# Column order and placement of the operands of the feed-forward matmuls

## The reference, cut to what matters

```
D_MODEL = 2048; SEQ = 512; D_FF = 5632
h = rms_norm(x, norm_ffn[layer])
x = x + (jax.nn.silu(h @ w_gate[layer]) * (h @ w_up[layer])) @ w_down[layer]
return rms_norm(x, norm_final)
```

## Time and profile before

| | |
|---|---|
| median of the runs of the kernel before | 2104.19 us (2 runs, 2094.29 to 2114.09) |
| the profiled execution, its own time | 2099.91 us |
| its span in the trace | 2098.2 us |
| mean granted TensorE clock | 0.99 |
| TensorE matmul busy | 2040.7 us (97%) |
| VectorE busy | 1566.1 us (75%) |
| ScalarE busy | 956.3 us (46%) |

### The profile page before, as it was taken

One profiled execution on the slowest core, in us unless ns is written; L12 is line 12 of the kernel. 1 busy time (PEld: TensorE's weight loads), 2 busy tenths in 40 slices (PEclk: granted clock), 3 DMA queues, 4 the chain that ended last, 5 costly groups with the idle time before them and its releaser, 6 DMA issues.

```text
span 2098.2 us, 32169 instructions
## 1 busy us (share of the span) xinstructions
PE 2040.7 (97%) x13205; PEld 1817.0 (87%) x13205; DVE 1566.1 (75%) x2106; ACT 956.3 (46%) x1476; POOL 277.1 (13%) x153
## 2 busy tenths in 40 slices
PE   8999999999979999999999999999999999999998
PEld 6888777777658889999999999999999988888886
DVE  6723566777762227888898889889888898988995
ACT  5222356667652227544444444444444433333343
POOL 4000011211120000123113203203203100000002
PEclk9999999999989999999999999999999999999999
DMA  7671222211035334335446445345345755665622
GB/s 262 217 208 61 61 66 56 61 56 53 13 121 186 115 121 140 102 131 179 154 141 198 134 159 192 122 157 185 131 147 186 301 194 188 228 213 181 236 106 81
DMA packets 197779, 306.46 MB, mean 146 GB/s; under 512 B 8640, under 2 KB 121344, under 8 KB 192512
## 3 DMA queue, kind: packets, MB, share of 16 engines
q1 hardware_dynamic: 197600, 304.38, 43.6%
q10 hardware_dynamic: 32, 0.01, 0.0%
HBM read 248.79 MB, written 55.57 MB: 145 GB/s over the span
## 4 chain that ended last, share of the span: by engine, by line
PE 88%; DVE 6%; issue 3%; ACT 2%; DMA 0%; POOL 0%; DVEq 0%; ACTq 0%; POOLq 0%
PE bank L2641 11%; PE bank L2644 11%; PE bank L2646 11%; PE bank L2698 6%; PE bank L2696 6%; PE bank L2693 6%; PE bank L2242 3%; PE bank L2244 3%; PE bank L2243 3%; PE bank L2508 3%; PE bank L2510 3%; PE bank L2512 3%; PE bank L2408 3%; PE bank L2530 2%; PE bank L2534 2%
## 5 line engine op out<-in xcount | busy, mean ns | idle before, releaser
L1297 ACT ACTIVATE w_all<-raw 128x1024 fp32r<-128x1024 f32 x292 | 305.6, 1058 | 279.6 <-PE bank L2698 156.9
L1891 DVE TENSOR_TENSOR w_all<-raw,w_all 128x1024 fp32r<-128x1024 f32 x292 | 378.0, 1306 | 71.5 <-ACT w_all L1297 71.0
L2641 PE MATMUL bank<-x_T,w_all 128*128 128x256 f32 x1344 | 373.2, 278 | 0.0
L2646 PE MATMUL bank<-x_T,w_all 128*128 128x256 f32 x1344 | 373.2, 278 | 0.0
L2644 PE MATMUL bank<-x_T,w_all 128*128 128x256 f32 x1344 | 373.2, 278 | 0.0
L2641 PE MATMUL bank<-x_B,w_all 128*128 128x256 f32 x1008 | 280.9, 279 | 0.8 <-DVE w_all L1891 0.2
L2644 PE MATMUL bank<-x_B,w_all 128*128 128x256 f32 x1008 | 279.9, 278 | 0.0
L2646 PE MATMUL bank<-x_B,w_all 128*128 128x256 f32 x1008 | 279.9, 278 | 0.0
L2641 PEld LDWEIGHTS bank<-x_T,w_all 128*128 128x128 f32 x1344 | 254.2, 189 | 0.0
L2644 PEld LDWEIGHTS bank<-x_T,w_all 128*128 128x128 f32 x1344 | 252.3, 188 | 0.0
L2646 PEld LDWEIGHTS bank<-x_T,w_all 128*128 128x128 f32 x1344 | 252.3, 188 | 0.0
(11 more groups left out here) (299 smaller groups left out, 4394.3 us busy)
## 6 DMA issues: line engine op xcount, KB each, us to landing
raw<-in_w_gate SPq DMA_DIRECT2D x39, 1024.0 KB, 5.1
h_scratch<-late SPq DMA_DIRECT2D x70, 512.0 KB, 3.1
raw<-in_w_down SPq DMA_DIRECT2D x50, 512.0 KB, 5.2
proj_q<-in_w_up SPq DMA_DIRECT2D x22, 1024.0 KB, 6.8
raw<-in_w_up SPq DMA_DIRECT2D x22, 1024.0 KB, 7.9
x_B<-h_scratch SPq DMA_DIRECT2D x20, 1024.0 KB, 5.0
raw<-in_w_in SPq DMA_DIRECT2D x16, 1024.0 KB, 10.4
raw<-in_w_out SPq DMA_DIRECT2D x16, 1024.0 KB, 5.5
```

The source lines that it names most:

```text
L1297: nc.scalar.activation(piece_hi(p), piece_raw(n, k), ACT.Copy).then_inc(piece_hi_done, 1)
L1891: nc.vector.tensor_tensor(piece_lo(p), piece_raw(n, k), piece_hi(p).bitcast(F32), ALU.subtract).then_inc(piece_lo_done, 1)
L2641: nc.tensor.matmul(dst, wh[:, t, cs], x_lo(x)[:, cols], start=start and part == 0 and t == 0 and a == 0, stop=False, skip_group_check=True)
L2646: done = nc.tensor.matmul(dst, wh[:, t, cs], x_hi(x)[:, cols], start=False, stop=part == 1 and t == 3, skip_group_check=True)
```

## The change

`X_AT` gets a value of its own for each activation operand, and `h_flat(r)` a shift `H_AT[r]`. The accumulators of `sums` move from column 0 to column 128 of their halves, and so does the low part of the last down products. Two tables give each product an order in which the streamed columns are read; the PSUM columns are written in the same order, so each result stays in its place. Of every 256 or 512 columns, "lines" takes 16 from the first half, 16 from the second, then the next 16 of the first, and so on; "far" takes 16 from each of four quarters in turn; "halves" takes 8 from each half in turn; "plain" is the order of before. `first_piece`, `last_down` and all else keep the plain order; `first_piece` reads the operands at their new places. The number of instructions is the same.

```
-        X_AT = dict.fromkeys(x_names, 48)
+        X_AT = {"B11": 32, "T1": 0, "B21": 16, "T2": 48, "T3": 48, "B22": 64, "T4": 32}
+        X_ORDER = {"B11": "lines", "T1": "lines", "B21": "lines", "T2": "lines", "T3": "plain",
+                   "B22": "far", "T4": "halves"}
+        H_AT = [0, 96, 64, 112, 0, 96, 80]
+        H_ORDER = ["lines", "lines", "far", "lines", "plain", "halves", "lines"]
+
+        def streamed(cols, order):
+
+            if order == "lines":
+                return cols.rearrange("p (h j c) -> p j h c", h=2, c=16)
+            if order == "far":
+                return cols.rearrange("p (h j c) -> p j h c", h=4, c=16)
+            if order == "halves":
+                return cols.rearrange("p (h j c) -> p j h c", h=2, c=8)
+            return cols
...
         def h_flat(r):
-            return half_of(xc, H_HOME[r][0], H_HOME[r][1], 0)
+            return half_of(xc, H_HOME[r][0], H_HOME[r][1], H_AT[r])
...
         def sums(name, half):
-            return half_of(x_plain, name, half, 0).rearrange("p (q i c) -> p q i c", q=2, i=2)
+            return half_of(x_plain, name, half, 128).rearrange("p (q i c) -> p q i c", q=2, i=2)
...
-        last_lo = [half_of(xc, "T4", 1, 0), h_flat(1), h_flat(3), h_flat(5)]
+        last_lo = [half_of(xc, "T4", 1, 128), h_flat(1), h_flat(3), h_flat(5)]
...
                         for a in range(2):
-                            cs, dst = slice(P * a, P * (a + 1)), bank[:, HALF_TOK * a:HALF_TOK * (a + 1)]
-                            nc.tensor.matmul(dst, wh[:, t, cs], x_lo(x)[:, cols],
+                            cs = slice(P * a, P * (a + 1))
+                            order = X_ORDER[x]
+                            dst = streamed(bank[:, HALF_TOK * a:HALF_TOK * (a + 1)], order)
+                            xl, xh = (streamed(v[:, cols], order) for v in (x_lo(x), x_hi(x)))
+                            nc.tensor.matmul(dst, wh[:, t, cs], xl,
...
-                            nc.tensor.matmul(dst, wl[:, t, cs], x_hi(x)[:, cols], start=False,
+                            nc.tensor.matmul(dst, wl[:, t, cs], xh, start=False,
...
-                            done = nc.tensor.matmul(dst, wh[:, t, cs], x_hi(x)[:, cols], start=False,
+                            done = nc.tensor.matmul(dst, wh[:, t, cs], xh, start=False,
...
                             h_hi, h_lo = (h_operand(r)[:, s, 2 * part + t, toks] for s in range(2))
-                            nc.tensor.matmul(dst[:, :], h_lo, wh[:, t, :],
+                            order = H_ORDER[r]
+                            dst = streamed(dst[:, :], order)
+                            ml, mh = (streamed(w[:, t, :], order) for w in (wl, wh))
+                            nc.tensor.matmul(dst, h_lo, mh,
...
-                            nc.tensor.matmul(dst[:, :], h_hi, wl[:, t, :], start=False, stop=False,
+                            nc.tensor.matmul(dst, h_hi, ml, start=False, stop=False,
...
-                            done = nc.tensor.matmul(dst[:, :], h_hi, wh[:, t, :], start=False,
+                            done = nc.tensor.matmul(dst, h_hi, mh, start=False,
```

## The result

The changed kernel takes 2153.55 us (median of 2 runs, 2151.69 to 2155.41) against 2104.19 us before (2094.29 to 2114.09): a ratio of 1.0208, 95% interval 1.0133 to 1.0283. It is slower by about 50 us; the interval doesn't reach 1, but takes in both sides of the 2% line. The forecast of 2100 us with its range up to 2132 us was wrong.

The account below looks back on a forecast made before the run. The prediction took TensorE's matmul pitch to bound gate and up and down. New places and new order, 0 + 0 us on the profiled 2099.9 us, gave 2100 us, range 2056 to 2132 us (8 in 10).

Parts of the forecast that it names:

- What bounds the kernel: Gate and up and down: TensorE's matmuls fill the time, so a change of pitch moves the end by its full size.
- the rival of the vanished extra: Streamed columns, six of seven products: runs from far places remove the extra cycle per 16 columns; 40 us less, 2060 us; chance 0.23.
- the bounds of the order: Reordered streams, six of seven products in each stage: from 40 us less to 70 us more, with 0 us taken.
- a fixed price doesn't ask what came before: Reordered streams: one cycle per 16 columns is a fixed fetching price, so runs of 16 cost as now; 0 us taken.
- each jump costs a cycle: Rival, streams of six products in seven: every jump costs its own cycle; 70 us more, 2170 us; chance 0.20.
- The cost of the new places: New operand shifts: no instruction added, only the share at 113.3 or 117.8 ns can move; 0 us, bounds -11 and +21.
- extra cycle goes: Reordered streams: the extra cycle per 16 columns disappears; 40 us less, 2060 us; chance 0.23.
- The two steps: Gate and up: pitches 113.3 and 117.8 ns, a gap sets which; rival all in one, 2089 or 2121 us, chance 0.13.

Follow-up runs that it names:

- order_only: Changed kernel with the new column orders on the old places (activation operands at 48, hidden operands at 0): 2152.23 us, ratio to before 1.0177.
- parity: Changed kernel on old places, reading runs of 16 columns at various steps per product (0 +1: each run twice), PSUM written plainly, output not the layer's: 2143.82 us.
- places_only: Changed kernel with the new places but every product in the plain order: 2133.18 us, ratio to before 1.0090.
- dst_only: Changed kernel with streamed columns read plainly and only PSUM written in the new orders, output not the layer's: 2134.50 us.
- all_112: Changed kernel with all orders plain, all activation operands at shift 112, hidden operands at 0: 2111.34 us, ratio to before 1.0031.
- reset_48: Changed kernel with all orders plain, activation operands at shift 48 but T2 at 80, hidden operands at 0: 2105.36 us, ratio to before 0.9969.
- one_reset: Changed kernel with all orders plain, activation operands at 80, 96, 112, 80, 48, 80, 48, hidden at 0: 2108.76 us, ratio to before 0.9973.
- reset_112: Changed kernel with all orders plain, activation operands at shift 112 but T2 at 96, hidden operands at 0: 2101.29 us, ratio to before 0.9941.
- before_again: The kernel of before, unchanged, run and traced once more: 2098.18 us.

## Why the prediction was wrong, point by point

- **What bounds the kernel** was right: TensorE fills both stages, and the pitch went into the time (+32 and +18 us in the stages, +52 in the span). One thing was read too lightly: the seven waits of 2.2 us in all belong to gaps like the one above. At 113.3 ns VectorE, busy for 88% of the stage, already holds TensorE up in every second group. A still shorter pitch would hardly have reached the end whole, as the rival of the vanished extra assumed.
- **The step that failed** is the choice between the bounds of the order: "a fixed price doesn't ask what came before". The price of one cycle in 16 is not fixed. It is the best case of a supply that depends on which columns came before: the same runs of 16 took 120.0 and 240.0 ns in lines (order_only), two cycles in 16 and not one. I had measured nothing but that best case. All streams of the kernel before went on by one run of 16, so their even share could not tell a fixed price from a favourable order. The row that did point to a tight supply (the extra vanishing at 1.2 GHz) was read rightly and then weighed too little: the jumps had a chance of 0.20.
- **The rival "each jump costs a cycle"** named the side and the place, with 70 us for the 50 measured. Its mechanism is refuted all the same: steps of 48 and 80 columns jump at pitches that plain columns have, runs of 64 too, and (4, 8) costs less than (4, 16). In lines its 120 and 240 ns were exact, and in part by luck: every second step of lines goes on by an even number of runs, and other streams with such a step every second time (0 +1 and 1 2 of parity) take 120 and 240 ns too, while in gate and up steps of 80 columns alone paid nothing; for runs of 8 it said 127 and 253, and 123.3 and 243.2 came; for far 120 and 240, and 117.6 and 231.1 came.
- **The sum of that rival**, 70 us, was too large for a second reason too: it laid 6.7 ns on the stretches at 117.8 as well, while a stream in lines runs at 120.0 in every trace, so those matmuls lost 2.2. The measured stages give 50.5 us.
- **The cost of the new places** was bounded by -11 and +21 us in gate and up and put at nothing in down. places_only shows +23.6 and +5.4 in the plain order. The bounds knew two pitches; there are more (118.7, 119.9), and the stationary operand's shift counts as the streamed one's does. In the changed kernel this price is nearly covered by that of the order; it is seen in B22 (117.6, and 120.1 on the old place). T3, unmoved and plain, ran at 117.8 in all groups there and at 113.3 in nearly all of order_only.
- **The rival "extra cycle goes"** is refuted as far as it was tried: of more than fifty pairs of order and shift in the two stages none is under 113.3 or 226.7 ns.
- **The two steps**: that gaps choose between them was right for equal shifts. That a product at another shift can choose as well was not foreseen.
- **Two rules that the prediction named.** The Trainium skill ("PSUM — Partial Sum Buffer", section "Specifications (TRN2)") says that any PSUM pattern that isn't contiguous slows matmuls markedly. dst_only disagrees for whole runs of 8 and 16 columns: the pitches are those of plain writes within 0.1 ns. The Trainium skill ("SBUF — State Buffer", section "Who interferes with whom") says that the two read ports of the engine are independent and that it never waits on anyone. The runs disagree: moving the stationary operand alone took 512 streamed columns from 226.7 to 233.2 ns, though its load has room (matmuls with a full load each follow at 111.4 ns). That the two reads hold each other up is the likely reading.

## What to carry to other kernels

Where float32r matmuls are back to back at the full clock, read the pitch to a tenth of a nanosecond and compare it with columns over clock. What was over it here went with the order of the streamed columns and with the place of an operand. At the lower clock neither the plain order nor lines had anything over it. Leave streamed columns contiguous, or in runs of 64 and more (runs of 32 took 233.3 and 236.7 ns in down, not 226.7), and try shifts of one operand by 16 columns before anything else; a shift costs no instruction. If the same kernel spreads more than its neighbours, look for small gaps that come from the second busiest engine: they can change the pitch of all that follows. A price read off rows that all have the same form bounds the price of another form from one side only.

## What the runs showed of the hardware that I had not expected

- Streams of float32r columns at 2.4 GHz take 17 cycles for 16 columns at best (113.3 ns for 256, 226.7 for 512), and 18 in many other orders (120.0, 240.0); at 1.2 GHz both orders take one cycle per column.
- The price goes with the shift of the activation operand modulo 64 columns (256 bytes), by up to 5.8% in gate and up and 3.4% in down, and the best shift of the one is not that of the other. Whether its distance from the weights counts, or its own place, is open.
- Going on by 3 or 5 runs of 16 is as cheap as going on by one in gate and up (117.8 and 113.3 ns, both of them pitches of plain columns); by 0, 2, 4 or 8 runs costs a cycle per run (120.0). In down +3 is dear (237.8), in a pattern with one more dimension than in gate and up. What decides is open.
- With the same program and the same shifts a stream of 256 columns has two stable pitches, 113.3 and 117.8 ns, exchanged at a gap or at the border to a product at another shift or in another order. The single runs of kernels that can stay in either step spread by 32 us (before, by chip 9 to 32), 29 (all_112) and 22 (reset_48), those of kernels with fixed pitches by 3 to 5 (order_only, places_only, one_reset, reset_112). An estimate from the trace of before_again: its some 6,600 matmuls at 113.3 ns, all at 117.8, are 30 us more, less 3 us for eight gaps that go, so some 27 of those 32 us.
